# Down products of the first MLP: rests of the second half's weights by an adding DMA, and two more pairs by seven products

## The reference, cut to what matters

```python
h = rmsnorm(x, norm_mlp)
x = x + jnp.square(jax.nn.relu(h @ w_up)) @ w_down     # w_up 1024x4096, w_down 4096x1024
# second block: the next thing that needs x
h = rmsnorm(x, norm_mix_2);  h @ w_in_2 ...
```

## Time and profile before

| | |
|---|---|
| median of three runs | 954.05 us |
| the profiled execution | 953.48 us |
| its span in the profile | 951.3 us |
| TensorE busy | 943.1 us (99%) |
| VectorE busy | 701.3 us (74%) |
| ScalarE busy | 558.4 us (59%) |
| GpSimd busy | 128.5 us (14%) |
| DMA | 170.43 MB, mean 179 GB/s |

### The profile page before, as it was taken

One profiled execution on the slowest core, in us unless ns is written; L12 is line 12 of the kernel. 1 busy time (PEld: TensorE's weight loads), 2 busy tenths in 40 slices (PEclk: granted clock), 3 DMA queues, 4 the chain that ended last, 5 costly groups with the idle time before them and its releaser, 6 DMA issues. The chain is left out here.

```text
span 951.3 us, 16977 instructions
## 1 busy us (share of the span) xinstructions
PE 943.1 (99%) x6888; PEld 868.2 (91%) x6888; DVE 701.3 (74%) x934; ACT 558.4 (59%) x852; POOL 128.5 (14%) x178
## 2 busy tenths in 40 slices
PE   9999999999999999999999999999999999999997
PEld 7877999989999999989987999998998899999996
DVE  6767875777777887888866787776666467777777
ACT  6577554556666666656865674545455445555544
POOL 3000001004223320414000001100000012121210
PEclk9999999999999999999999999999999999999999
DMA  9974447555666666656565365555645346565661
GB/s 309 305 242 130 118 128 179 159 177 185 191 190 194 194 195 202 181 160 199 146 188 162 106 202 175 176 182 172 196 162 171 118 156 201 176 201 177 199 200 66
DMA packets 133549, 170.43 MB, mean 179 GB/s; under 512 B 5824, under 2 KB 97296, under 8 KB 133472
## 3 DMA queue, kind: packets, MB, share of 16 engines
q1 hardware_dynamic: 131408, 165.07, 55.9%
q10 hardware_dynamic: 1424, 2.84, 0.9%
q0 software_dynamic: 640, 1.44, 0.7%
HBM read 168.28 MB, written 1.05 MB: 178 GB/s over the span
## 5 line engine op out<-in xcount | busy, mean ns | idle before, releaser
L1661 DVE TENSOR_TENSOR parts<-raws,parts 128x1024 fp32r<-128x1024 f32 (+3 forms) x307 | 364.5, 1202 | 131.3 <-ACT parts L1111 130.4
L1111 ACT ACTIVATE parts<-raws 128x1024 fp32r<-128x1024 f32 (+3 forms) x307 | 309.3, 1029 | 129.2 <-PE ps L405 54.2
L403 PE MATMUL ps<-room_r,parts 128*128 128x256 f32 x1248 | 351.6, 282 | 0.0
L404 PE MATMUL ps<-room_r,parts 128*128 128x256 f32 x1248 | 348.6, 279 | 0.0
L405 PE MATMUL ps<-room_r,parts 128*128 128x256 f32 x1248 | 348.3, 279 | 0.0
L403 PEld LDWEIGHTS ps<-room_r,parts 128*128 128x128 f32 x1248 | 234.6, 188 | 2.2 <-issue 0.8
L404 PEld LDWEIGHTS ps<-room_r,parts 128*128 128x128 f32 x1248 | 234.7, 188 | 1.1
L405 PEld LDWEIGHTS ps<-room_r,parts 128*128 128x128 f32 x1248 | 234.7, 188 | 0.0
L434 PE MATMUL ps<-parts,room_r 128*128 128x512 f32 (+1 forms) x336 | 133.9, 399 | 0.8 <-DVE parts L1661 0.8
L435 PE MATMUL ps<-parts,room_r 128*128 128x512 f32 (+1 forms) x336 | 131.1, 390 | 0.0
L436 PE MATMUL ps<-parts,room_r 128*128 128x512 f32 (+1 forms) x336 | 131.1, 390 | 0.0
(11 more groups left out here) (241 smaller groups left out, 1115.1 us busy)
## 6 DMA issues: line engine op xcount, KB each, us to landing
raws<-in_w_in SPq DMA_DIRECT2D x99, 512.0 KB, 4.4
raws<-in_w_ffn_in SPq DMA_DIRECT2D x44, 512.0 KB, 4.4
raws<-in_w_up SPq DMA_DIRECT2D x32, 512.0 KB, 3.9
raws<-in_w_down SPq DMA_DIRECT2D x32, 512.0 KB, 3.8
raws<-in_w_ffn_out SPq DMA_DIRECT2D x22, 512.0 KB, 4.4
raws<-in_w_xkv SPq DMA_DIRECT2D x16, 512.0 KB, 4.4
raws<-in_w_out SPq DMA_DIRECT2D x8, 512.0 KB, 4.3
raws<-in_w_up_ssd SPq DMA_DIRECT2D x8, 512.0 KB, 5.5
```

Of the source, the lines that this page charges most:

```text
L403: e.matmul(ps, wh, hT[0][:, k, :], start=k == 0, stop=False)
L404: e.matmul(ps, wh, hT[1][:, k, :], start=False, stop=False)
L1111: e.activation(t.h, t.raw, ACT.Copy).then_inc(s["hi"], 1)
L1661: e.tensor_tensor(t.l, t.raw, t.h.bitcast(F32), ALU.subtract).then_inc(s["lo"], 1)
```

## The change

Three things are edited.

First, the right half of w_down in the first MLP, d', leaves the ring of `parts`. Its tile for pairs 1 to 15 has three buffers of its own (`weight_sent`). ScalarE rounds it into h and then writes minus h into l (`sent_rounded`). GpSimd then issues a DMA that reads the weights once more from memory and adds them onto l (`send`), so that l becomes raw minus h. VectorE has no part in it. The raw slot is free as soon as h is written. The load is asked for ahead of `up(q)` instead of behind `down(q-2, 0)`.

Second, pairs 0 and 14 of `down(q, 0)` are made by seven products as well, so that pairs 0 to 14 are.

Third, in `residual` of the second block, VectorE takes its tiles in between only where their place is released before the tail (`due_rest`).

The order in the scalar program for one q is now (for q = 1 and 2 the sums are rounded behind the copy instead): until, `sums_rounded(0, q-1)`, `sent_rounded(q-2)` (the tile of pair q-1), relu, square, copy; and behind the loop `sent_rounded(14)` (the tile of pair 15), then `first_copied`.

```diff
-        by_sums = [range(1, 14), range(1, 10)]
+        by_sums = [range(15), range(1, 10)]
+        at_sent = (10240, 12288, 24576)
...
+            def weight_sent(src):
+                slot, at = len(loaded) % RAW, at_sent[len(sent) % 3]
+                raw = chunks(raws[:, slot, :], 2)
+                h, l = (chunks(room_r[:, i:i + 1024], 2) for i in (at, at + 1024))
+                t = Tile(None, [(raw, src.rearrange("(k p) n -> p k n", p=P))], 2, 512, raw, h, l)
+                t.slot, t.before = slot, loaded[-RAW]
...
+                    if h and q in asked:
+                        w_ = asked[q]
+                        need(s[f"sent_lo{(w_.nth_sent - 1) % 3}"], 16 * ((w_.nth_sent - 1) // 3 + 1))
...
                 for q in range(2, n):
+                    if q > 2:
+                        ask(q - 2)
                     up(q)
                     down(q - 2, 0)
                     if q < n - 1:
                         down(q - 2, 1)
+                ask(n - 2)
                 down(n - 2, 0)
+                ask(n - 1)
                 down(n - 1, 0)
...
+            def sent_rounded(n):
+                t = sent[n]
+                e.wait_ge(landed[t.slot], t.load)
+                if n >= 3:
+                    e.wait_ge(s["pe"], sent[n - 3].release)
+                e.activation(t.h, t.raw, ACT.Copy).then_inc(s["sent_hi"], 1)
+                e.wait_ge(s["sent_hi"], n + 1)
+                e.activation(t.l, t.h.bitcast(F32), ACT.Copy, scale=-1.0).then_inc(s["sent_minus"], 1)
             def up(q):
                 until(where["up", q].at)
-                sums_rounded(0, q - 1)
+                if q > 2:
+                    sums_rounded(0, q - 1)
+                if q > 1:
+                    sent_rounded(q - 2)
                 full(("up", q))
...
             for q in range(16):
                 up(q)
+            sent_rounded(14)
             first_copied(0)
...
+            def due_rest(u):
+                if gives_back(lo) < where["tail", u].at:
+                    rest_of_tile()
...
+            def send(n):
+                t = sent[n]
+                e.wait_ge(s["sent_minus"], n + 1)
+                e.dma_start(t.l, t.srcs[0][1].bitcast(F32R), accum_op=ALU.add).then_inc(s[f"sent_lo{n % 3}"], 16)
             def all_up_sums(u):
                 for q in by_sums[u]:
+                    if u == 0 and q > 1:
+                        send(q - 2)
```

More of the change, by code:

```diff
@@ L47 @@
     "ret_sq", "ret_rstd", "ret", "oT_hi", "retT_hi", "gates", "mix", "mix_hi", "mixT", "up", "up_hi", "upT",
-    "qk_hi", "qk", "w_sums", "u_sums", "us_hi", "usT", "first_product", "joined",
+    "qk_hi", "qk", "w_sums", "u_sums", "us_hi", "usT", "first_product", "joined", "sent_hi", "sent_minus",
+    "sent_lo0", "sent_lo1", "sent_lo2",
     "pad", "conv_in", "conv", "silu", "gated", "Aexp", "dt", "soft_e", "soft_exp", "soft_sq", "soft", "a", "a_twice", "narrow", "sel", "cs_hi", "decays", "X", "Xd", "E",
@@ L66, in __init__ @@
         self.slot = self.load = self.before = None
-        self.sums = self.nth_sums = None
+        self.sums = self.nth_sums = self.nth_sent = None
         self.release = None
@@ L307, in build @@
         where = {}
-        tiles, loaded, made = [], [], []
+        tiles, loaded, made, sent = [], [], [], []
         def gives_back(i):
@@ L369, in weight @@
                 loaded.append(t)
+                return t
+            def weight_sent(src):
[4 more added lines that the diff above has]
+                t.slot, t.before = slot, loaded[-RAW]
+                t.load = 16 + t.before.load
+                sent.append(t)
+                loaded.append(t)
+                t.nth_sent = len(sent)
                 return t
@@ L782, in down_by_sums @@
                     product(p1, u11, w11, first)
-                    product(c11, u12, w21)
+                    product(c11, u12, w21, first and q == 0)
                     need(s["usT"], nth_sums[u][q] + 1)
@@ L793, in down_by_sums @@
                         ends(last, ("product", u, 1), sums_in[1])
-                    sums.release = done(product(c21, u22, t4))
+                    sums.release = done(product(c21, u22, t4, first and q == 0))
                 def down(q, h):
@@ L799, in down @@
                         return down_by_sums(q)
-                    w_ = weight(w_down[256 * q:256 * q + 256, 512 * h:512 * h + 512], 2, 512)
-                    need(s["lo"], w_.i + 1)
+                    if h and q in asked:
+                        w_ = asked[q]
+                        need(s[f"sent_lo{(w_.nth_sent - 1) % 3}"], 16 * ((w_.nth_sent - 1) // 3 + 1))
+                    else:
+                        w_ = weight(w_down[256 * q:256 * q + 256, 512 * h:512 * h + 512], 2, 512)
+                        need(s["lo"], w_.i + 1)
                     for t in range(2):
@@ L805, in down @@
                             wh, wl, (uh, ul) = w_.h[:, k, :], w_.l[:, k, :], ups[q % 4]
-                            e.matmul(ps, uh[:, k, tok], wh, start=q == 0 and k == 0, stop=False)
+                            if h == 0 and t and k == 0 and q == by_sums[u][-1] + 1 and 0 in by_sums[u]:
+                                for c in (slice(0, 256), slice(256, 512)):
+                                    e.matmul(ps[:, c], uh[:, k, tok], wh[:, c], start=False, stop=False)
+                            else:
+                                e.matmul(ps, uh[:, k, tok], wh, start=q == 0 and k == 0, stop=False)
                             e.matmul(ps, uh[:, k, tok], wl, start=False, stop=False)
@@ L813, in down, with ask @@
                         where["down", u, q] = Group(None, count, None)
+                asked = {}
+                def ask(q):
+                    if u == 0:
+                        asked[q] = weight_sent(w_down[256 * q:256 * q + 256, 512:D])
                 for q in range(2, n):
+                    if q > 2:
+                        ask(q - 2)
                     up(q)
@@ L1399, in up @@
                 e.activation(ups[q % 4][0], r, ACT.Copy).then_inc(s["up_hi"], 1)
+                if q in (1, 2):
+                    sums_rounded(0, q - 1)
             for q in range(16):
                 up(q)
+            sent_rounded(14)
             first_copied(0)
@@ L1781, in residual @@
                 if late:
-                    rest_of_tile()
+                    due_rest(u)
                 gains(u, 0, late)
                 if late:
-                    rest_of_tile()
+                    due_rest(u)
                 rests(u, 0)
                 if late:
-                    rest_of_tile()
+                    due_rest(u)
                 for t in range(2):
@@ L2061, in vector @@
                 until(where[name].at)
-                sums_rest(0, q - 1)
+                if q > 2:
+                    sums_rest(0, q - 1)
                 full(name)
@@ L2499, in gpsimd @@
             all_up_sums(0)
+            for n in (13, 14):
+                send(n)
             e.wait_ge(s["xT"], 4 * MIX2 + 4)
@@ L2580, in sync @@
                 if t.before:
-                    e.wait_ge(s["lo"], t.before.i + 1)
+                    if t.before.nth_sent:
+                        e.wait_ge(s["sent_hi"], t.before.nth_sent)
+                    else:
+                        e.wait_ge(s["lo"], t.before.i + 1)
                     if t.before.sums:
```

## The result

The changed kernel takes 979.35 us (median of 4 runs, 976.68 to 981.71) against 953.85 for the kernel before (median of 4 too). The ratio is 1.0264, 95% interval 1.025 to 1.0278: 25.5 us slower. I had forecast slower by 6, with 963.8 as the upper end. The direction was right and the size was not.

What follows compares the result with a forecast made beforehand. TensorE's matmul list was taken as the bound; -0.66 + 0.3 + 4.7 + 0.1 + 1.6 = +6.0 on 953.48 gave 959.5, or 960.1 with the runs' median 0.57 higher; range 958.5 to 962, eight in ten 957.0 to 963.8.

Steps and rivals of the forecast that it cites:

- What bounds the kernel: Whole kernel: TensorE's matmul list sets the time; only fewer matmuls help (0.33 us per pair, 0.66 for two), only new waits hurt.
- The periods in the middle: Middle pairs of the first MLP: ScalarE finishes its added copies in time, so 0 lost (0 to 0.2 us per pair).
- The adding DMA: First MLP, each pair's right half: the DMA lands within its 11 us (bounds 5.3 and 9.7), so 0 cost.
- Rival 2: MLP middle: adding DMA costs 2.5 loads or more, DMA engines become the bound, waits in every pair; 969 to 973, chance 0.06.
- The first pairs: Start of the MLP: up(3)'s second tile is late, TensorE waits 0.2 us, 0.3 with refill (bounds 0 and 1.0).
- The end of the MLP: After up(15): d(15) is copied behind four copies, so TensorE waits 4.7 us for its rest (3.8 to 5.7), plus 0.1 refill.
- The join behind it: Transposes after the MLP's last pairs: a late c2 tile delays the additions, TensorE waits 1.6 us (0 to 3).
- rival 1: Gap at the MLP's end: clock falls to 1.2 GHz, +0.8 to +2.4 us more, 961 to 962.5; chance 0.32.

Runs made afterwards that it cites:

- Experiment 2: Changed kernel with the own-buffer tile's load asked for behind up(q) instead of ahead of it: 962.19 us, ratio 1.0089.
- experiment 1: Changed kernel without the 15 adding DMAs, TensorE waiting for the minus part instead (rests left out of the computation): 959.87 us, ratio 1.0063.
- experiment 4: Changed kernel without the sending (right half through the ring as before), pairs 0 and 14 still by seven products: 956.56 us, ratio 1.0029.
- experiment 8: Changed kernel without the sending, seven products for pairs 0 to 13 and pair 14 plain: 954.72 us, ratio 1.001.
- experiment 9: Changed kernel without the sending, seven products for pairs 0 to 13, VectorE's four residual tiles always taken as before: 953.04 us, ratio 0.9993.
- experiment 10: Changed kernel without the sending, seven products for pairs 0 to 14, VectorE's four residual tiles always taken as before: 955.15 us, ratio 1.0016.
- experiment 5: Changed kernel with the 15 adding DMAs made plain ones of the same bytes, queue and places (rests left out): 969.01 us, ratio 1.0149.
- experiment 11: Changed kernel, own-buffer loads asked behind up(q); in up(15) relu, square, copy, then d(15), then the four copies; both engines stop at d(15) before the join: 965.77 us.
- experiment 6: Changed kernel with own-buffer loads asked for behind up(q) and seven products only for pairs 1 to 13: 961.42 us, ratio 1.0076.
- experiment 3: Changed kernel with seven products only for pairs 1 to 13, as before the change, sending kept: 974.43 us, ratio 1.0218.
- experiment 7: Changed kernel, own-buffer loads asked behind up(q), seven products for pairs 0 to 13, pair 14's two copies made before d(15) in up(15): 958.53 us, ratio 1.005.

## Why the prediction was wrong

**What bounds the kernel** held: no matmul waited before, a pair by seven products still takes 2.48 where nothing is late, and 7 us less on VectorE bought nothing.

**The periods in the middle** failed. The step was "the ring looks a tile further ahead. So in steady state I count 0 (0 to 0.2 per pair, if loads come late)". It cost 15.2 by up(15). I followed the copies on ScalarE and gave the transfers the 4.4 of the earlier trace rows, whatever else was in flight. I did not write down what stands ahead of a load on SyncE. The diff says it: `ask` comes before `up`, and its load waits for a slot that ScalarE frees last. Experiment 2 shows that 17 us hang on this order. They hang on the adding DMA as much (experiment 1): in the bad order without it the middle loses nothing.

**The adding DMA** failed in the same place. The step was "both in time. I take 0". Its size was inside my bounds: 1.7 loads' worth of engine time (bounds 1 and 2), landing in 9.1 (bounds 5.3 and 9.7). The 11 us that it had were counted from 8.0, the moment at which ScalarE would write the minus part. In the period shown the copy is written 307.25 + 1.06 - 296.64 = 11.7 after the start of that up, so 3.7 late, and GpSimd is at the issue for 1.2 more. TensorE's row of that start:

```profile
296.64 0.28 PE L418 MATMUL ps<-room_r,parts 128*128 128x256 f32 x1
```

The two ends of a bound do not protect when the start of the interval is itself the thing that moves. Rival 2 named the sign that came true, waits in every pair, and came nearest in size (969 to 973, measured 979), but its reason was wrong and its nearness luck. It wanted full DMA engines on average, from 2.5 loads on; they were at 0.82 and the DMA cost 1.7 loads. It got 0.06.

**The first pairs**: 0.3 forecast; after, a wait of 0.5 in up(3), which takes 0.8 longer. That is inside the bounds.

**The end of the MLP** held in kind and size: 4.7 forecast, 4.96 measured, by the path written down. The kernel without the DMA has just this wait and comes out at 959.87. **The join behind it**: 1.6 forecast, 0.7 measured, because rival 1 came true too: the clock fell in the gap and took 1.9. What I did not see is that ScalarE comes 2.3 late into the end (s(14) at 7.7 after the start of up(15), not 5.4), which gives 0.4 and 1.0 in pair 14's products. In experiments 1 and 2 s(14) is at 6.1 and 6.0 and these waits are absent, so the loop accounts for 1.6 of it; the other 0.7 my steps had too short. The page "TensorE: Matmul & The Clock Gate" of the Trainium skill, in its section "HAM oscillation — how this bites in real kernels", has an idle gap re-throttle the engine; the trace agrees, 0.50 from 396 on.

**The third edit** I passed over ("I see nothing late in the second block"). In the changed kernel that came true. Without the sending the edit costs 1.4 to 1.7 (experiments 4 and 8 to 10).

## What to carry to other kernels

When a load moves forward in a queue, list what its slot waits for and what stands behind it in that queue; if the engine that frees the slot does so behind a tile that comes through that same queue, the two form a loop, and its length against the period of the bound engine is the number to work out. A landing time from a row holds for the crowd it was measured in: count the transfers in flight together, not their average share. And an engine with a quarter of its time free has that free time in places; the end of a stage, where the order changes, has to be written out by itself.

## What the runs showed of the hardware

- A DMA that adds float32 from memory onto the on-chip tile took 1.7 times the DMA engine time of a plain one of the same 512 KB (2.9 against 1.7 us of all 16 engines, after against experiment 5); the plain one from GpSimd's queue cost as much as a load from SyncE (1.7).
- In experiment 11 a 512 KB load from SyncE issued at 378.1 landed after 3.7 us; one issued at 380.15, as the third of four loads and with both adding DMAs about it, landed after 11.1 us.
- GpSimd was busy 1.20 us to issue one such DMA, 0.94 for each of the small ones in the earlier trace rows.
- The clock fell to the lower level in gaps of 5.0 (after, experiments 1 and 2) and stayed at 0.50 through some 4 us of plain matmuls after it; it also fell behind shorter ones. In experiment 6 the matmuls stand 0.43 apart from 379.03 on, behind a gap of 2.3 that begins at 375.9, and in experiment 3 from 269.42 on, behind one of 2.1. In experiment 7, with a gap of 2.4, the clock was 1.00 through and behind it. I had read only the end of the kernel before (2.9) as its measure, and in the kernel after it fell 2.2 after the last matmul; what parts these cases stays open.
